# Dilated attention moved between the retention's projections, retention moved to the end, in the first mixers of a two-model kernel

## The chip, the cores and the metric

The kernel runs on one core of one Trainium2 chip, as one program with one launch. The metric is device time in microseconds, the median of several executions. The core has five engines that work side by side, each through its own instructions in program order, tied together by semaphores: TensorE (PE in the profile, matrix products; its weight loads are PEld), VectorE (DVE), ScalarE (ACT), GpSimd (POOL) and SyncE (SP), which here issues the DMAs.

## The reference

Two transformer models run one after the other on a sequence of 512 tokens of width 1024. The first has two layers (feed-forward, token mixer, feed-forward), the second two further layers of other kinds. The change touches the first model's token mixer alone, which runs twice, once in each layer:

```python
def _token_mixer(h, w_in, w_out):
    proj = h @ w_in
    rq, rk, rv, rg, dq, dk, dv, sq, sk, sv = jnp.split(proj, points, axis=-1)
    y_ret = _retention(_rotate(rq), _rotate(rk), rv, rg)      # 4 heads, 64 x 128
    y_dil = _dilated_attention(_rotate(dq), _rotate(dk), dv)  # 4 heads of 64
    y_sb = _stick_breaking(sq, sk, sv)                        # 4 heads of 64
    return jnp.concatenate([y_ret, y_dil, y_sb], -1) @ w_out
```

Retention is a decayed causal product without softmax, its output normed over each head's 128 columns and multiplied with `silu(rg)`. Dilated attention is a softmax over masked scores. Stick-breaking weights each value by running sums of log-sigmoids. All of it is in float32.

## The kernel before

Activations lie transposed, as eight tiles of 128 features by 512 tokens. Each large product is made of three passes, since both factors are parted into a high and a low half (`HH` and `HL` for the activations; ScalarE copies the high half, VectorE or GpSimd subtracts for the low one). Weights come in chunks of 256 columns: a DMA into a stage, the high half copied by ScalarE (`split`), the low one subtracted by VectorE (`low`). One chunk gives 48 products of 512 columns on TensorE.

The order of all work is written by a planner, class `Plan`, in plain Python before anything is emitted. It makes one list of steps; each engine's program is that list with the steps that concern it. Background work is written as generators ("units"): a unit yields between its steps. `self.tick()`, called after each half tile of a projection (12 products), starts up to `burst` new units from the queue `bg`, if fewer than `depth` are active, then waits `pace` ticks before it starts more, and moves every active unit one step on. A callable at the head of `bg` holds the queue until it gives true. `pipeline` ticks until all is done, with no projection between; `until(f)` ticks until `f()` holds.

`first_mixer` goes so. `late` makes the projections `sq` and `sk`; then follow the projection `sv`, and stick-breaking units in pairs of heads (`sb_z`, `sb_keep`, `sb_sum`, `sb_mask`, `sb_av`), one every second tick, beside `rq`, `rk` and `rv`. Then the gates `rg` (chunks 4 and 5), `dq`, `dk` and `dv` are projected, with eight retention units (`ret_s`, `ret_av`) and the retention's norm (`ret_norm`: squares `ret_sq`, column sums `ret_var`, root `ret_rs`, and for each head `ret_out`, which spreads the root over a PSUM bank and multiplies it in) beside them. Last, `self.pipeline(dil_units())` runs the 16 dilated units (`attend`: score and mask, `at_exp`, `at_norm`, `at_turn`, `at_av`), two a tick. Then `m_part` parts the tiles 6, 7 (stick-breaking) and 0 to 3 (retention); tiles 4 and 5 (dilated) are parted directly from PSUM by the last `at_av`. `project_out` makes the product with `w_out`, whose first chunk takes the eight tiles in the order 6, 7, 0 to 5, two per call of `mm2`. Its `take` also writes the split of the next weight chunk and, at this place, one chunk of the modulation's rows (`ada_rows`, VectorE, L2150 to L2156).

Lines of the profile: L1487 is every TensorE product, L1502 the spread, L1507 the transpose; L1814 every plain copy of ScalarE; L2137 `low`; L2130 and L2691 low halves of `HL` on VectorE and GpSimd; L2106 to L2125 the root; L2369 and L2760 the two multiplications of `ret_out` on VectorE and GpSimd; L1955 `ret_sq`; L2742 and L2755 the masks of `sb_keep` and `sb_mask`; L2402 `at_norm`.

Of the kernel before, what the change touches and what calls it, by code (L numbers as in the profile page):

```python
# [25 lines left out]
P = 128  # L26
# [79 lines left out]
class Plan:  # L106
# [216 lines left out]
                self.tick()  # L323
        return b, self.pid

    def feat2(self, ch, kt, x, ver, eager=False, n=S, order=None):
# [4 lines left out]
        yield from self.rest_of(*self.begin(ch, kt, n, x, ver, order))  # L331

    def begin(self, ch, kt, n, x, ver, order=None, wide=(P, P)):
        bs = [self.banks.take(), self.banks.take()]
        self.pid += 2
        return ch, self.pid - 1, kt, n, bs, x, ver, list(order or range(kt)), wide

    def rest_of(self, ch, pid, kt, n, bs, x, ver, ks, wide):

        for i in range(0, kt, 2):  # L340
            self.add("mm2", pid, ch, kt, n, bs, x, ver, ks, wide, i, i + 2)
            self.tick()
        yield bs[0], pid
        yield bs[1], pid + 1
# [279 lines left out]
            self.hv += 1  # L624
        return after or (total if mean != "rms" else self.squares(*total))

    def project_out(self, name, idx0, kt, nc, x, ver, gate, mean, order=None, nxt=None, raw=None):
        total, done, per = (self.new(), []), [], nc // P
        after = self.norm(*nxt) if nxt else None
        for c in range(NT // per):  # L630
            ch = self.take(name, idx0 + c, ada=c == 0)
            tiles = (self.feat2(ch, kt, x, ver, True, order=order) if per == 2 and c == 0 else
                     (self.feat(ch, kt, nc, t, x, ver) for t in range(per)))
# [40 lines left out]

    def first_mixer(self, l, norm):
        extra = [("xm", i) for i in range(3)]
        nk_done, sb_done, out_done, ropes = {}, [], {}, []

        def proj(idx, key):
            ch = self.take("w_in", l * 12 + idx, ada=False)  # L680
# [66 lines left out]
        def ret_unit(pr, j, cells):  # L747
            b, q = [], []
            for c in range(2):
                b.append(self.banks.take())  # L750
                q.append(self.tmp.take())
                self.banks.free(b[c], ("ret.d", l, 2 * pr + c, j))
            self.add("ret_s", l, pr, j, b, q)
            yield
            for c in range(2):
                if j == 0:
                    cells.append(self.held.take())
                self.add("ret_av", l, 2 * pr + c, j, cells[c], q[c])
                self.tmp.free(q[c], ("ret.o", l, 2 * pr + c, j))
                if j == 3:  # L760
                    self.held.free(cells[c], ("ret.kept", l, 2 * pr + c))
                    out_done[2 * pr + c] = True

        def ret_norm():
            yield
            st2 = self.held.take()
            prev = None
            for h in range(5):
                if h < 4:
                    q = self.tmp.take()  # L770
                    self.add("ret_sq", l, h, q)
                if prev is not None:
                    self.add("ret_var", l, h - 1, st2, prev)
                    self.tmp.free(prev, ("ret.var", l, h - 1))
                prev = q
                if h % 2:
                    yield
            y = self.yr.take()
            self.add("ret_rs", l, st2, y)
            self.held.free(st2, ("rs.v", "ret%d" % l))  # L780
            yield
            yield
            for h in range(4):
                b = self.banks.take()
                self.add("ret_out", l, h, y, b)
                self.banks.free(b, ("ret.out", l, h))
                yield
            self.yr.free(y, ("ret.sp2", l, 3))

        def ret_units():  # L790
# [3 lines left out]
                    yield ret_unit(pr, j, cells)  # L794
            yield ret_norm()

        def setpace(n):
            self.pace = n
            return True

        def dil_units():
            for pr in range(2):
                cell = []
                for i in range(4):
                    for c in range(2):
                        yield self.attend("dil", l, 2 * pr + c, i, (i + 1) * P, cell, i == 3 and c == 1)
# [8 lines left out]
        for i in extra:  # L815
            self.tmp.after[i] = [free]
        self.tmp.ids += extra
        tproj(11, "sv", 0)
        self.bg.extend(sb_units())
        self.pace = 2  # L820
        proj(0, "rq")
        proj(1, "rk")
        self.active += [roped("rq", "ret"), roped("rk", "ret")]
        tproj(2, "rv", 0)
        tproj(3, "rv", 256)
        self.bg.append(lambda: setpace(1))
        self.bg.append(lambda: len(ropes) >= 2 and len(sb_done) == 2)
        self.bg.extend(ret_units())
        for c in range(2):
            ch = self.take("w_in", l * 12 + 4 + c, ada=False)  # L830
            for t in range(2):
                b, pid = self.feat(ch, 8, 256, t, "h", hv, turn=False)
                self.add("m_gate", l, 2 * c + t, pid, b)
                self.banks.free(b, ("m.g", l, 2 * c + t))
                self.tick()
            self.release(ch, ("proj", pid))
        proj(6, "dq")
        proj(7, "dk")
        self.active += [roped("dq", "dil"), roped("dk", "dil")]
        self.hfree = tproj(8, "dv", 0)  # L840
        self.hv += 1
        self.burst, self.depth = 2, 8
        self.bg.append(lambda: len(ropes) == 4)
        self.pipeline(dil_units())
        self.burst, self.depth = 1, 6
# [10 lines left out]
    def attend(self, kind, l, h, i, n, cell, last, free=None):  # L856

        u = (kind, l, h, i)
        b, q, sm = self.banks.take(), self.tmp.take(), self.small.take()
# [19 lines left out]
        if last:  # L879
            o = cell[0]  # L880
            if kind == "x":
                self.held.free(o, ("o.lo", l, h), ("o.hi", l, h))
            else:
                self.held.free(o, ("h.lo", self.hv, 4 + h // 2), ("h.hi", self.hv, 4 + h // 2))

# [924 lines left out]
def scalar(e, m, plan):  # L1810
    act = e.i

    def copy(out, src):
        return act.activation(out, src, ACT.Copy)  # L1814
# [103 lines left out]
    def m_gate(l, h, pid, b):  # L1918
        e.wait_ge(("proj", pid))
        act.activation(m.t["rg"][:, h, :], m.bank(b), ACT.Silu).then_inc(*e.up("act_evict", "m.g", l, h))  # L1920

    def sb_z(l, pr, j, z, q):
# [32 lines left out]
        act.activation(m.tmp(q), m.ret(h), ACT.Square).then_inc(*e.up("act_sq", "ret.sq", l, h))  # L1955

    def m_part(l, n, odd, hv, hfree):
        e.wait_ge(("sb.kept", l, n - 6) if n >= 6 else ("ret.out", l, n), hfree)
        copy(m.HH[:, n, :], m.mixed(n)).then_inc(*e.up("act_h", "h.hi", hv, n))


# [11 lines left out]
    def at_av(u, n, p, o, last, hv, hfree):  # L1973
        if last and u[0] == "x":
            e.wait_ge(("at.o", u), hfree)
            copy(m.OH[:, u[2], :], m.bank(o)).then_inc(*e.up("act_h", "o.hi", u[1], u[2]))
        elif last:
# [119 lines left out]
def vector(e, m, plan):  # L2097
# [248 lines left out]
    def m_center(l, i, c0):  # L2346
        v = m.t["rv"][:, i:i + 2, c0:c0 + 256].rearrange("p a (g n) -> p a g n", n=P)
        total = m.RM[:, 0:4].rearrange("p (a g) -> p a g", a=2)
        e.wait_ge(("m.v", l, "rv", c0, i))
# [54 lines left out]
    def at_av(u, n, p, o, last, hv, hfree):  # L2404
        if last and u[0] == "x":
            e.wait_ge(("o.hi", u[1], u[2]))
            dve.tensor_tensor(m.OL[:, u[2], :], m.bank(o), m.OH[:, u[2], :].bitcast(F32), ALU.subtract).then_inc(
                *e.up("dve_h", "o.lo", u[1], u[2]))
        elif last:
            h_low(hv, 4 + u[2] // 2, m.bank(o))  # L2410


# [433 lines left out]
class Mem:  # L2846
# [105 lines left out]
    def first_mixer(self):  # L2952
        at = self.parts(("sq", [2, S]), ("sk", [2, S]), ("sv", [4, 256]), ("rq", [2, S]), ("rk", [2, S]), ("nk", [2, 1280]),
                        ("rv", [4, S]), ("rg", [4, S]), ("dq", [2, S]), ("dk", [2, S]), ("dv", [4, 256]))
        self.spare("xm", 3, at)

    def even_mixer(self):
        at = self.parts(("qi", [2, S]), ("ki", [S]), ("bm", [1152]), ("wi", [4, 4]), ("st", [4, 18]),
# [83 lines left out]
        return self.t["nk"][:, :, :].rearrange("p a n -> p (a n)")[:, h * S:(h + 1) * S]  # L3042

    def mixed(self, n):
        return self.t["rg"][:, n, :] if n < 4 else self.t["sq"][:, n - 6, :]

    def tile(self, key, t):
        if key == "ki":
# [209 lines left out]
```

## Time and profile before

| | |
|---|---|
| runs | 3520.28, 3524.86, 3524.43 us; median 3524.43 |
| profiled execution | 3520.2 us from the first to the last instruction; no time beside the span is given for it |
| TensorE busy | 3433.7 us, 98% |
| VectorE, ScalarE, GpSimd busy | 1894.9, 1198.5 and 519.9 us |
| chain that ended last | TensorE 34% of the span, nearly all of it L1487 |

A busy share near 100% on one engine means that the length of its own instructions sets the time. Matmul durations overlap in the records, since they are pipelined: the distance from start to start is what one costs (0.23 us for 512 columns at the full clock, 0.43 at half). PEclk is the granted clock as a share of 2.4 GHz.

### The profile page before, as it was taken

To read this page: it belongs to the slowest core of one execution; us is meant where nothing else is said; L and a number is where in the kernel's file an instruction comes from. 1 tells how busy PE (TensorE), PEld (TensorE's weight loads), DVE (VectorE), ACT (ScalarE), POOL (GpSimd) and SP (SyncE) were. 2 spreads that over 40 slices of the span, in tenths; PEclk is the share of its full clock that TensorE was granted. 3 is DMA by queue.
4 is the path that set the end of the run, shared out by engine and by line. 5 is a ranking of instruction groups with operands and counts; after the bars stand their busy time and mean duration, and the time that the engine had idled before them with its cause. 6 is when DMAs were issued, how large, how long until landed. Compare 5 with 4: busy or idle time off the path is not lost. (4 is left out here: it accounts for less than half of the span.)

```text
span 3520.2 us, 40510 instructions
## 1 busy us (share of the span) xinstructions
PE 3433.7 (98%) x16478; PEld 2789.2 (79%) x16478; DVE 1894.9 (54%) x3227; ACT 1198.5 (34%) x1646; POOL 519.9 (15%) x454
## 2 busy tenths in 40 slices
PE   8999999999999999999999999989999999999999
PEld 5888876688888888876788877757888888878887
DVE  5555753664556455744752346885643345564433
ACT  3222352442224222453442234445432222352221
POOL 1010231210012010231210021112011110211111
PEclk9999999999999999999999999979999999999999
DMA  6444221133442444211132212101222222322221
GB/s 264 178 180 179 92 77 60 49 144 144 168 144 108 155 156 161 93 58 48 63 142 96 96 66 84 60 13 61 73 96 96 96 96 99 108 73 96 96 96 72
DMA packets 53036, 372.53 MB, mean 106 GB/s; under 512 B 6001, under 2 KB 6129, under 8 KB 10098
## 3 DMA queue, kind: packets, MB, share of 16 engines
q1 hardware_dynamic: 52850, 369.94, 28.8%
q8 instruction: 130, 2.13, 0.2%
q14 instruction: 56, 0.46, 0.0%
HBM read 367.82 MB, written 2.10 MB: 105 GB/s over the span
## 5 line engine op out<-in xcount | busy, mean ns | idle before, releaser
L1487 PE MATMUL ps<-s_hh,s_wh 128*128 128x512 f32 x2552 | 1012.8, 397 | 18.8 <-POOL s_hl L2691 14.1
L1487 PE MATMUL ps<-s_hh,s_wl 128*128 128x512 f32 x2552 | 998.3, 391 | 0.0
L1487 PE MATMUL ps<-s_hl,s_wh 128*128 128x512 f32 x2552 | 998.0, 391 | 0.0
L2137 DVE TENSOR_TENSOR s_wl<-s_stage,s_wh 128x2048 fp32r<-128x2048 f32 (+1 forms) x276 | 623.5, 2259 | 635.3 <-ACT s_wh L1814 635.3
L1814 ACT ACTIVATE s_wh<-s_stage 128x2048 fp32r<-128x2048 f32 (+1 forms) x276 | 519.2, 1881 | 586.0 <-PE ps L1487 427.0
L1487 PEld LDWEIGHTS ps<-s_hh,s_wh 128*128 128x128 f32 x2552 | 481.7, 189 | 138.9 <-issue 34.9
L1487 PEld LDWEIGHTS ps<-s_hh,s_wl 128*128 128x128 f32 x2552 | 481.7, 189 | 102.7
L1487 PE MATMUL ps<-s_ah,s_wh 128*128 128x512 f32 x1408 | 561.9, 399 | 0.7 <-POOL s_al L2730 0.7
L1487 PEld LDWEIGHTS ps<-s_hl,s_wh 128*128 128x128 f32 x2552 | 482.5, 189 | 98.0 <-issue 0.7
L1487 PE MATMUL ps<-s_ah,s_wl 128*128 128x512 f32 x1408 | 550.1, 391 | 0.0
L1487 PE MATMUL ps<-s_al,s_wh 128*128 128x512 f32 x1408 | 549.5, 390 | 0.0
L2730 POOL TENSOR_TENSOR s_al<-s_tmp,s_ah 128x512 fp32r<-128x512 f32 x152 | 197.5, 1303 | 1665.9 <-ACT s_ah L1814 1665.9
L1487 PEld LDWEIGHTS ps<-s_ah,s_wl 128*128 128x128 f32 x1408 | 264.3, 188 | 57.4
L1487 PEld LDWEIGHTS ps<-s_ah,s_wh 128*128 128x128 f32 x1408 | 264.6, 188 | 54.9 <-POOL s_al L2730 1.6
L1487 PEld LDWEIGHTS ps<-s_al,s_wh 128*128 128x128 f32 x1408 | 264.7, 188 | 53.6 <-issue 1.9
L1814 ACT ACTIVATE s_ah<-s_tmp 128x512 fp32r<-128x512 f32 x152 | 95.9, 632 | 562.0 <-DVE s_tmp L2320 302.8
L2197 DVE TENSOR_TENSOR s_xr<-ps,s_xr 128x512 f32<-128x512 f32 x96 | 66.1, 689 | 196.8 <-PE ps L1487 196.8
L2153 DVE SCALAR_TENSOR_TENSOR s_tmp<-s_stage,s_cond,s_tmp 128x256 f32<-128x256 f32 x384 | 157.3, 478 | 0.0
L2195 DVE SCALAR_TENSOR_TENSOR s_xr<-ps,s_sm,s_xr 128x512 f32<-128x512 f32 x112 | 83.0, 748 | 114.1 <-PE ps L1487 113.5
L1842 ACT ACTIVATE s_tmp<-ps 128x512 f32<-128x512 f32 x82 | 48.8, 596 | 251.4 <-PE ps L1487 251.4
L2320 DVE TENSOR_TENSOR s_tmp<-s_tmp,ps 128x512 f32<-128x512 f32 x82 | 55.6, 684 | 113.1 <-PE ps L1487 111.8
L2304 DVE TENSOR_TENSOR s_tmp<-ps,s_c 128x512 f32<-128x512 f32 x64 | 44.0, 688 | 118.5 <-PE ps L1487 105.1
(502 smaller groups left out, 3614.7 us busy)
## 6 DMA issues: line engine op xcount, KB each, us to landing
s_stage<-in_w_ada SPq DMA_DIRECT2D x64, 1024.0 KB, 4.8
s_stage<-in_ffn_w_gate SPq DMA_DIRECT2D x44, 1024.0 KB, 4.8
s_stage<-in_ffn_w_up SPq DMA_DIRECT2D x44, 1024.0 KB, 4.8
s_stage<-in_ffn_down SPq DMA_DIRECT2D x32, 1024.0 KB, 4.8
s_stage<-in_w_up SPq DMA_DIRECT2D x32, 1024.0 KB, 4.7
s_stage<-in_down_m SPq DMA_DIRECT2D x32, 1024.0 KB, 4.7
s_stage<-in_w_in SPq DMA_DIRECT2D x24, 1024.0 KB, 4.8
s_stage<-in_ffn_down SPq DMA_DIRECT2D x16, 768.0 KB, 4.3
```

The source lines that it names most:

```text
L1487: return pe.matmul(out, lhs, rhs, start=start, stop=stop, skip_group_check=True)
L1814: return act.activation(out, src, ACT.Copy)
L1842: act.activation(m.tmp(q), m.bank(b), ACT.Silu).then_inc(*e.up("act_ffn", "act", pid))
L2137: ins = dve.tensor_tensor(m.wl(ws)[:, a:z], m.STAGE[:, j % NS, a:z], m.wh(ws)[:, a:z].bitcast(F32), ALU.subtract)
L2153: ins = dve.scalar_tensor_tensor(dst, w[:, k, :], cond, dst, ALU.mult, ALU.add)
L2195: ins = dve.scalar_tensor_tensor(x, m.bank(b), m.small(gate[0])[:, n:n + 1], x, ALU.mult, ALU.add)
L2197: ins = dve.tensor_tensor(x, m.bank(b), x, ALU.add)
L2304: dve.tensor_tensor(x, m.bank(b), m.RB, ALU.mult).then_inc(*e.up("dve_act", "act", pid))
L2320: dve.tensor_tensor(m.tmp(q), m.tmp(q), m.bank(b), ALU.mult).then_inc(*e.up("dve_ffn", "glu", pid))
L2730: pool.tensor_tensor(m.AL[a][:, k, :], m.tmp(q), m.AH[a][:, k, :].bitcast(F32), ALU.subtract).then_inc(*e.up("pool_a", "a.lo", av, k))
```

## The change

The mixer's projections are reordered to `sv`, `dq`, `dk`, `dv`, `rq`, `rk`, `rv`, gates. The dilated units start beside `rq`, at two a tick; the retention units beside the gates; the retention's norm is run after the last gate product. The output product's first chunk takes the tiles in the order 6, 7, 4, 5, 0, 1, 2, 3, and `rest_of` waits in the plan for each pair to be parted. The gates' space serves as four more temporaries until the gates are written. A retention cell takes a rotating PSUM bank where no held one is free. The dilated output is copied to `dq` and parted later.

```diff
-    def rest_of(self, ch, pid, kt, n, bs, x, ver, ks, wide):
+    def rest_of(self, ch, pid, kt, n, bs, x, ver, ks, wide, ready=None):
         for i in range(0, kt, 2):
+            if ready:
+                self.until(lambda: ready(ks[i]) and ready(ks[i + 1]))
             self.add("mm2", pid, ch, kt, n, bs, x, ver, ks, wide, i, i + 2)
             self.tick()
...
                 if j == 0:
-                    cells.append(self.held.take())
+                    ring = self.held if self.held.spare() else self.banks
+                    cells.append((ring, ring.take()))
...
+            rooted.append(y)
             yield
             yield
             for h in range(4):
                 b = self.banks.take()
                 self.add("ret_out", l, h, y, b)
                 self.banks.free(b, ("ret.out", l, h))
-                yield
+                self.add("m_part", l, h, h % 2, self.hv, self.hfree)
+                parted.append(h)
+                if h % 2:
+                    yield
...
         tproj(11, "sv", 0)
         self.bg.extend(sb_units())
-        self.pace = 2
+        self.depth = 5
+        proj(6, "dq")
+        proj(7, "dk")
+        self.active += [roped("dq", "dil"), roped("dk", "dil")]
+        tproj(8, "dv", 0)
+        self.bg.append(lambda: len(ropes) >= 2 and pacing(1, 2, 9))
+        self.bg.extend(dil_units())
         proj(0, "rq")
         proj(1, "rk")
         self.active += [roped("rq", "ret"), roped("rk", "ret")]
         tproj(2, "rv", 0)
         tproj(3, "rv", 256)
-        self.bg.append(lambda: setpace(1))
-        self.bg.append(lambda: len(ropes) >= 2 and len(sb_done) == 2)
+        self.bg.append(lambda: len(ropes) == 4 and len(sb_done) == 2 and len(dil_done) >= 1 and pacing(1, 1, 9))
         self.bg.extend(ret_units())
...
-        proj(6, "dq")
-        proj(7, "dk")
-        self.active += [roped("dq", "dil"), roped("dk", "dil")]
-        self.hfree = tproj(8, "dv", 0)
+        self.hfree = ("proj", pid)
         self.hv += 1
-        self.burst, self.depth = 2, 8
-        self.bg.append(lambda: len(ropes) == 4)
-        self.pipeline(dil_units())
-        self.burst, self.depth = 1, 6
-        order = (6, 7, 0, 1, 2, 3, 4, 5)
-        for i, n in enumerate(order[:6]):
+        self.until(lambda: len(dil_done) == 2)
+        order = (6, 7, 4, 5, 0, 1, 2, 3)
+        for i, n in enumerate(order[:4]):
             self.add("m_part", l, n, i % 2, self.hv, self.hfree)
+        self.until(lambda: rooted)
...
         norm = self.project_out("w_out", l * 4, 8, 256, "h", self.hv, gate, "ln", order,
-                                (l, 1, (l, 6, 7), None))
+                                (l, 1, (l, 6, 7), None), ready=lambda n: n in parted or n >= 4)
+        self.pace, self.burst, self.depth = 1, 1, 6
```

`pacing(pace, burst, depth)` sets the three and gives true. `attend` gets a list `done`, to which a dilated pair of heads adds itself at its last unit.

## Rows read from the trace of the kernel before

**Rows 1.** The page, part 1: TensorE's busy time and instructions.

```profile
PE 3433.7 (98%) x16478; PEld 2789.2 (79%) x16478; DVE 1894.9 (54%) x3227; ACT 1198.5 (34%) x1646; POOL 519.9 (15%) x454
```

**Rows 2.** Table of windows of 50 us: busy of each engine, clock, DMA.

```profile
600.00:650.00 50.00, 42.26 (x290) 30.80 (x289) 35.20 (x93) 26.16 (x62) 14.58 (x10) 0.93 0.06 22
...
1650.00:1700.00 50.00, 42.55 (x251) 30.38 (x250) 36.77 (x97) 26.33 (x62) 9.35 (x6) 0.93 0.12 43
...
2700.00:2750.00 50.00, 50.00 (x223) 41.38 (x222) 17.89 (x17) 9.70 (x7) 2.59 (x2) 1.00 0.30 106
```

**Rows 3.** TensorE's waits, 451.9 to 658.8 us: total, times, longest.

```profile
PE ps L1507 <- DVE s_tmp L2402: 3.4, 3, 2.2
PE ps L1487 <- POOL s_hl L2691: 2.6, 1, 2.6
PE ps L1487 <- POOL s_xm L2755: 2.1, 1, 2.1
```

**Rows 4.** Timeline of TensorE, dilated stage: start, duration, operation, [idle before <- releaser].

```profile
617.05 1.03 PE L1502 MATMUL ps<-s_cc,s_ny 128*128 128x128 f32 x8
...
621.57 0.72 PE L1507 MATMUL ps<-s_cc,s_tmp 128*128 128x128 f32 x2 [2.20 <-DVE s_tmp L2402]
...
636.51 1.13 PE L1487 MATMUL ps<-s_dk,s_dq 64*128 64x512 f32 x4
...
641.49 0.65 PE L1507 MATMUL ps<-s_cc,s_tmp 128*128 128x128 f32 x4
642.07 2.23 PE L1487 MATMUL ps<-s_tmp,s_dv 128*64 128x128 f32 x28
646.95 0.77 PE L1487 MATMUL ps<-s_hh,s_wh 128*128 128x512 f32 x1 [2.65 <-POOL s_hl L2691]
```

**Rows 5.** Timeline of TensorE, the retention's norm beside the projection `dk`.

```profile
590.47 1.05 PE L1487 MATMUL ps<-s_cc,s_tmp 128*128 128x1 f32 x8 [1.21 <-ACT s_tmp L1955]
591.38 0.48 PE L1487 MATMUL ps<-s_hh,s_wh 128*128 128x512 f32 x1
...
595.81 1.84 PE L1487 MATMUL ps<-s_cc,s_tmp 128*128 128x1 f32 x16
597.51 0.47 PE L1487 MATMUL ps<-s_hh,s_wh 128*128 128x512 f32 x1
...
600.36 0.95 PE L1487 MATMUL ps<-s_cc,s_tmp 128*128 128x1 f32 x8
```

**Rows 6.** Timeline around a late stick-breaking mask: GpSimd, VectorE, TensorE.

```profile
528.59 0.46 POOL L2742 TENSOR_TENSOR s_nk<-s_nk,s_cc 128x128 f32<-128x128 f32 x1 [2.49 <-DVE s_tmp L2337]
529.91 2.43 POOL L2742 TENSOR_TENSOR s_nk<-s_nk,s_cc 128x128 f32<-128x128 f32 x1 [0.87 <-DVE s_tmp L2337]
...
529.75 2.28 DVE L2137 TENSOR_TENSOR s_wl<-s_stage,s_wh 128x2048 fp32r<-128x2048 f32 x1
...
532.81 1.33 PE L1487 MATMUL ps<-s_xm,s_sv 128*64 128x384 f32 x4 [2.05 <-POOL s_xm L2755]
```

**Rows 7.** Timeline of VectorE: root, multiplication, weight half, modulation's rows.

```profile
601.35 0.18 DVE L2106 TENSOR_SCALAR s_nv<-ps 128x16 f32<-128x16 f32 x1 [14.75 <-PE ps L1487]
...
603.45 0.17 DVE L2125 SCALAR_TENSOR_TENSOR s_ny<-s_nu,s_ny 128x16 f32<-128x16 f32 x1
...
607.65 0.69 DVE L2369 TENSOR_TENSOR s_rg<-s_rg,ps 128x512 f32<-128x512 f32 x1 [1.82 <-PE ps L1502]
...
651.56 2.28 DVE L2137 TENSOR_TENSOR s_wl<-s_stage,s_wh 128x2048 fp32r<-128x2048 f32 x1
653.77 0.61 DVE L2150 TENSOR_SCALAR s_tmp<-s_stage,s_cond 128x256 f32<-128x256 f32 x2
...
656.78 0.42 DVE L2156 TENSOR_TENSOR s_tmp<-s_tmp 128x256 f32<-128x256 f32 x1
```

**Rows 8.** Timeline of ScalarE: the retention's four squares.

```profile
589.79 2.18 ACT L1955 ACTIVATE s_tmp<-s_nk 128x512 f32<-128x512 f32 x4
```

**Rows 9.** Timeline of GpSimd: one gate product of the retention.

```profile
568.01 1.28 POOL L2760 TENSOR_TENSOR s_rg<-s_nk,s_rg 128x512 f32<-128x512 f32 x1 [26.72 <-ACT s_nk L1814]
```

More of the change, by code:

```diff
@@ L324, in feat, with feat2 @@
         return b, self.pid
-    def feat2(self, ch, kt, x, ver, eager=False, n=S, order=None):
+    def feat2(self, ch, kt, x, ver, eager=False, n=S, order=None, ready=None):
         if not eager:
@@ L330, in feat2 @@
             return
-        yield from self.rest_of(*self.begin(ch, kt, n, x, ver, order))
+        yield from self.rest_of(*self.begin(ch, kt, n, x, ver, order), ready)
     def begin(self, ch, kt, n, x, ver, order=None, wide=(P, P)):
@@ L625, in ffn, with project_out @@
         return after or (total if mean != "rms" else self.squares(*total))
-    def project_out(self, name, idx0, kt, nc, x, ver, gate, mean, order=None, nxt=None, raw=None):
+    def project_out(self, name, idx0, kt, nc, x, ver, gate, mean, order=None, nxt=None, raw=None, ready=None):
         total, done, per = (self.new(), []), [], nc // P
@@ L631, in project_out @@
             ch = self.take(name, idx0 + c, ada=c == 0)
-            tiles = (self.feat2(ch, kt, x, ver, True, order=order) if per == 2 and c == 0 else
+            tiles = (self.feat2(ch, kt, x, ver, True, order=order, ready=ready) if per == 2 and c == 0 else
                      (self.feat(ch, kt, nc, t, x, ver) for t in range(per)))
@@ L676, in first_mixer @@
         extra = [("xm", i) for i in range(3)]
-        nk_done, sb_done, out_done, ropes = {}, [], {}, []
+        gates = [("xg", i) for i in range(4)]
+        sb_done, dil_done, out_done, ropes, rooted, parted = [], [], {}, [], [], []
         def proj(idx, key):
@@ L756, in ret_unit @@
                 if j == 0:
-                    cells.append(self.held.take())
-                self.add("ret_av", l, 2 * pr + c, j, cells[c], q[c])
+                    ring = self.held if self.held.spare() else self.banks
+                    cells.append((ring, ring.take()))
+                ring, cell = cells[c]
+                self.add("ret_av", l, 2 * pr + c, j, cell, q[c])
                 self.tmp.free(q[c], ("ret.o", l, 2 * pr + c, j))
                 if j == 3:
-                    self.held.free(cells[c], ("ret.kept", l, 2 * pr + c))
+                    ring.free(cell, ("ret.kept", l, 2 * pr + c))
                     out_done[2 * pr + c] = True
@@ L795, in ret_units, with pacing @@
             yield ret_norm()
-        def setpace(n):
-            self.pace = n
+        def pacing(pace, burst, depth):
+            self.pace, self.burst, self.depth = pace, burst, depth
             return True
@@ L805, in dil_units @@
                     for c in range(2):
-                        yield self.attend("dil", l, 2 * pr + c, i, (i + 1) * P, cell, i == 3 and c == 1)
+                        yield self.attend("dil", l, 2 * pr + c, i, (i + 1) * P, cell, i == 3 and c == 1, None, dil_done)
         one, two, free = self.late(norm, (("w_in", l * 12 + 9), ("w_in", l * 12 + 10)))
@@ L814, in first_mixer @@
         hv = self.hv
-        for i in extra:
+        for i in extra + gates:
             self.tmp.after[i] = [free]
-        self.tmp.ids += extra
+        self.tmp.ids += extra + gates
         tproj(11, "sv", 0)
         self.bg.extend(sb_units())
-        self.pace = 2
+        self.depth = 5
[5 more added lines that the diff above has]
+        self.bg.extend(dil_units())
         proj(0, "rq")
@@ L825, in first_mixer @@
         tproj(3, "rv", 256)
-        self.bg.append(lambda: setpace(1))
-        self.bg.append(lambda: len(ropes) >= 2 and len(sb_done) == 2)
+        self.bg.append(lambda: len(ropes) == 4 and len(sb_done) == 2 and len(dil_done) >= 1 and pacing(1, 1, 9))
         self.bg.extend(ret_units())
+        self.tmp.ids = [i for i in self.tmp.ids if i not in gates]
         for c in range(2):
@@ L832, in first_mixer @@
                 b, pid = self.feat(ch, 8, 256, t, "h", hv, turn=False)
-                self.add("m_gate", l, 2 * c + t, pid, b)
+                self.until(lambda: ("xg", 2 * c + t) not in self.tmp.busy)
+                self.add("m_gate", l, 2 * c + t, pid, b, self.tmp.after[("xg", 2 * c + t)])
                 self.banks.free(b, ("m.g", l, 2 * c + t))
@@ L851, in first_mixer, with attend @@
         norm = self.project_out("w_out", l * 4, 8, 256, "h", self.hv, gate, "ln", order,
-                                (l, 1, (l, 6, 7), None))
+                                (l, 1, (l, 6, 7), None), ready=lambda n: n in parted or n >= 4)
+        self.pace, self.burst, self.depth = 1, 1, 6
         self.small.free(gate[0], ("x", NT - 1, self.xv[NT - 1]))
         return norm
-    def attend(self, kind, l, h, i, n, cell, last, free=None):
+    def attend(self, kind, l, h, i, n, cell, last, free=None, done=None):
         u = (kind, l, h, i)
@@ L882, in attend @@
                 self.held.free(o, ("o.lo", l, h), ("o.hi", l, h))
+            elif kind == "dil":
+                self.held.free(o, ("dil.kept", l, h // 2))
+                done.append(h // 2)
             else:
@@ L1916, in m_tcopy, with m_gate @@
             *e.up("act_evict", "m.v", l, key, c0, i))
-    def m_gate(l, h, pid, b):
-        e.wait_ge(("proj", pid))
+    def m_gate(l, h, pid, b, free):
+        e.wait_ge(("proj", pid), free)
         act.activation(m.t["rg"][:, h, :], m.bank(b), ACT.Silu).then_inc(*e.up("act_evict", "m.g", l, h))
@@ L1957, in m_part @@
     def m_part(l, n, odd, hv, hfree):
-        e.wait_ge(("sb.kept", l, n - 6) if n >= 6 else ("ret.out", l, n), hfree)
+        e.wait_ge(("sb.kept", l, n - 6) if n >= 6 else ("dil.kept", l, n - 4) if n >= 4 else ("ret.out", l, n), hfree)
         copy(m.HH[:, n, :], m.mixed(n)).then_inc(*e.up("act_h", "h.hi", hv, n))
@@ L1976, in at_av @@
             copy(m.OH[:, u[2], :], m.bank(o)).then_inc(*e.up("act_h", "o.hi", u[1], u[2]))
+        elif last and u[0] == "dil":
+            e.wait_ge(("at.o", u))
+            copy(m.t["dq"][:, u[2] // 2, :], m.bank(o)).then_inc(*e.up("act_evict", "dil.kept", u[1], u[2] // 2))
         elif last:
@@ L2348, in m_center @@
         total = m.RM[:, 0:4].rearrange("p (a g) -> p a g", a=2)
-        e.wait_ge(("m.v", l, "rv", c0, i))
+        e.wait_ge(("m.v", l, "rv", c0, i), ("m.c", l, c0, 0) if i else ("m.c", l, 0, 2) if c0 else None)
         dve.tensor_reduce(total, v, AXX, ALU.add).then_inc(*e.up("dve_ret", "m.total", l, c0, i))
@@ L2408, in at_av @@
                 *e.up("dve_h", "o.lo", u[1], u[2]))
-        elif last:
+        elif last and u[0] == "b":
             h_low(hv, 4 + u[2] // 2, m.bank(o))
@@ L2955, in first_mixer @@
         self.spare("xm", 3, at)
+        for k in range(4):
+            self.extra["xg", k] = self.t["rg"][:, k, :]
     def even_mixer(self):
@@ L3044, in mixed @@
     def mixed(self, n):
-        return self.t["rg"][:, n, :] if n < 4 else self.t["sq"][:, n - 6, :]
+        return self.t["rg"][:, n, :] if n < 4 else self.t["dq"][:, n - 4, :] if n < 6 else self.t["sq"][:, n - 6, :]
     def tile(self, key, t):
```

## The prediction

> **What bounds the kernel now.** I read the page first. The TensorE row [rows 1] shows 98% busy: everywhere outside a few stages the time is the length of the row of matmuls, so a reordering can only win what TensorE loses now, as idle time or at the half clock. The table of 50 us windows says where that is: in most windows, as in the last one quoted, TensorE is busy for 50.00 of 50; the two that hold the dilated attention, one for each of the two first mixers, show 42.26 and 42.55 at a granted clock of 0.93 [rows 2]. TensorE's waits in the first mixer's stretch name the rest: softmax (`s_tmp` L2402), the low half of the mixed rows (`s_hl` L2691), one stick-breaking mask (`s_xm` L2755) [rows 3]. The two mixers' windows differ by 0.3 us of busy time [rows 2], so I work out one and double it.
>
> A ledger of what TensorE loses in a mixer before, beyond the work itself:
>
> - Dilated stage. It runs from 617.05 (two spreads of the retention, 1.0 us) to the first output product at 646.95: 29.9 us [rows 4]. Its own TensorE work: eight pairs of scores, 1.13 us at 512 columns and in proportion below, so (4+3+2+1)/4 x 1.13 x 2 = 5.7; 40 transposes at 0.65/4 = 6.5; 80 value records at 2.23/28 = 6.4; together 18.6. Lost: 29.9 - 1.0 - 18.6 = 10.3.
> - Retention norm. 1.2 us idle at 590.47, then twelve products take 4.43 us (591.38 to 595.81), where the next twelve take 2.85 (597.51 to 600.36) [rows 5]: the clock had fallen to its lower level after the gap, 1.6 more. Lost: 2.8.
> - Stick-breaking: 2.05 us idle [rows 6], and one slow piece like the one above, estimated at 1.6 too: 3.7.
>
> Sum 16.8 us a mixer, 33.6 in all: the most that the change could win, about 1%.
>
> **The change, part by part.** The planner gives one background turn ("tick") for each half tile of projection, twelve products, 2.85 us [rows 5]. I followed the ticks from the first tick after the late tiles.
>
> *Middle.* The value projection `sv` has ticks 1 to 4, `dq`, `dk`, `dv` 5 to 16, `rq`, `rk`, `rv` 17 to 32, the gates 33 to 40. With pace 1 and depth 5 (the scaling unit takes a place until tick 10) stick-breaking units start at ticks 5 to 8, 11, 12, 14 and 16. Dilated units start at 17, two a tick; the last value product falls at tick 31. The retention can start only when `rv` is queued, at 33, last unit at 40. So all 18.6 us of dilated work lie between products of `rq`, `rk` and `rv`. They are eight ticks of two units: TensorE has 2.85 us of product and 18.6/8 = 2.3 of dilated work in each, 5.2 in all. The window that holds the whole stage has VectorE busy for 35.20 us and ScalarE for 26.16 [rows 2], so by an upper bound 4.4 and 3.3 us a tick, below 5.2. The 10.3 us go away. The stick-breaking units, now one a tick, keep their chain; the bounds for their stall are 0, if the products of the next unit cover it, and 3.7 for each as before (a rival). Following the queues I get a slip of some tenths at one mask and set 0.3.
>
> Instruction counts stay, also the DMA issues and their order relative to the chunks; fewer switches of ScalarE's table are off TensorE's path. The copy of the dilated output to `dq` is new in place of the direct high/low copy, but it lies beside products: nothing. The four low halves beside the gates' end: same durations as before, and not the last to come (below).
>
> *Tail.* Here the retention norm has no projection beside it any more. Let T be the end of the last gate product. On TensorE follow value products, scores, value products of the last units: 1.8 us, ending at about T+2.4. ScalarE, in order: the gate 0.6, four `m_part` copies at 0.54 (the shape of the squares), two kept copies, four squares (2.18 for four) [rows 8]: the first square ends at T+4.3. Four statistics cost 0.9 + 1.7 + 0.8 = 3.4 [rows 5], so they end at T+7.8. Idle so far 2.6.
>
> Then two blocks of output products (tiles 6, 7 and 4, 5, ready long before): 5.5 us to T+13.3, two spreads to 14.2. Beside them VectorE does the root, 2.3 us [rows 7], to T+10.1, seven small coefficient instructions (about 1, estimated at 0.15 each from the root's), the low half of the next weight chunk 2.2, and the modulation's rows, 653.77 to 657.20, 3.4 [rows 7]: these are written by `take` ahead of `ret_out`, in the order of the program. So VectorE reaches the first `ret_out` only at T+16.7. What is queued behind those rows is the multiplication, and for it wait ScalarE's copy, GpSimd's low half, TensorE's product of tile 0. The chain: multiplication 0.7 [rows 7], copy 0.6, low half on GpSimd 1.28, by an instruction of its shape [rows 9], so tile 0 at T+19.4: idle 5.1. GpSimd's gate product for head 1 stands behind that low half: 1.28 + 0.7 + 0.6 + 0.7 (VectorE's own low half) give T+22.8, less 1.4 of product: idle 2.0. The spreads of heads 2 and 3 stand behind those products: 0.5 + 0.7 + 0.6 + 1.28, 2.2 idle beyond the spreads; then head 3 as head 1: 1.9. The block ends at T+32. Idle: 2.6 + 5.1 + 2.0 + 2.2 + 1.9 = 13.8.
>
> The clock: no row shows such a row of gaps. Below: it never falls, 0. Above: every piece of about 3 us of work runs slow, four at 1.6 = 6.4. The dilated stage before is the nearest, the window holding it at 0.93 [rows 2]; I take two pieces, 3.2.
>
> **Sum.** After: 13.8 + 3.2 + 0.3 = 17.3; before 16.8; +0.5 a mixer, +1 in both. Against the profiled execution, span 3520.2, that is 3521.2; the median of the runs stands 4.2 above that span, so 3525.4. The ledger leaves out small slow pieces after the old gaps (some 1 us a mixer, which the change removes), so I say 3524. In words: what is won in the middle is given back in the tail.
>
> **Rivals.**
>
> *Faster, the clock holds in the tail.* The gaps are 2 us with 1.4 us of product between; row 590.47 shows a drop after 1.2 us idle plus thin statistics, which speaks against it; that in the old stage only part of 30 us was slow speaks for it. Slow 0 and middle 0: 13.8 against 16.8 + 1, so -4 a mixer, -8: 3516. With the 5.1 gap shorter too, as the rows may come while the statistics still run, down to -8 a mixer: 3508.
>
> *Slower, masks late in the middle.* Before, the mask that stalled TensorE stood behind a GpSimd instruction of 0.46 us that took 2.43, at the same time as VectorE's weight low half of 2.28 [rows 6]. With pace 1 there is a mask each tick beside the same weight halves. Each such stall is 3.7. The tail alone is 17.0; slower by over 7 us needs 17.0 + 3.7n > 17.8 + 3.5, so two stalls a mixer decide. Two: +6.6 a mixer, 3538; one: 3530. Against it: where before only every second tick started a unit, the ticks between a sum and its value product now hold another unit's products too, which cover a mask.
>
> The Trainium skill, "SBUF — State Buffer", section "SBUF: two separate sides", has the pair of ports that VectorE and GpSimd share as an exclusive lock, by which a VectorE instruction with two SBUF inputs blocks GpSimd wholly while it lasts. The trace agrees (0.46 grew to 2.43, by about the 2.28 beside it). By it each mask that meets a weight half is 2 us late; without it, it would be on time, and this rival would have no mechanism.
>
> *The change doesn't do what it says:* dilated units not done by the end of the gates. The count gives nine ticks of slack; 2 in 100.
>
> **Chances.** Under 0.2% (7 us) a measurement of this kernel tells no difference. Forecast, within 0.2%: 0.38. Clock holds or a shorter tail, faster: 0.34. Slower: 0.28, of it masks 0.15, a tail with all pieces slow (+3.7 a mixer, 3531) 0.11, not hidden 0.02. The range takes in both bounds of the clock and two masks nearly: 3508 to 3537. The likeliest case's own range is 3518 to 3531.
>
> **What would show it.** In the profile after: no stretch without projections between `dv` and the gates, and TensorE busy over 95% there; retention records beside the gate products; then, from the last gate product, about 32 to 36 us to the end of the first output chunk, with a wait of 5 us for `s_hl` after the block of tiles 4 and 5 and three of 2 us. VectorE's modulation rows (L2153) directly before the first multiplication at L2369. If that first wait is below 2 us the tail is mis-sized and the kernel is faster; if a mask wait (L2755) appears more than once a mixer, the slower rival holds. What would make me wrong most easily is the tail: it is one chain through four engines, each link with about 0.1 us of latency that I read off but did not sum twice.

## The result, and the profile after

| | before | after |
|---|---|---|
| median of the runs, us | 3522.36 (3517.81 to 3524.86) | 3543.50 (3540.51 to 3547.82) |
| profiled execution, span, us | 3520.2 | 3539.2 |
| ratio of the medians | | 1.006, 95% interval 1.0048 to 1.0072 |

The kernel became 21 us slower; 3524 was forecast, with 3537 as the upper end. The median stands 4.3 us above the profiled span: each run's time is 1.3 us above its own span, and the profiled run was the shortest of the four. Before, the forecast's 4.2 us came about in the same way, from three runs; with the fourth run the median of before is 3522.36, 2.2 us above its profiled span.

Part 1 of the page of the kernel after, to be held against [rows 1]:

```profile
PE 3448.9 (97%) x16478; PEld 2796.5 (79%) x16478; DVE 1890.8 (53%) x3225; ACT 1190.3 (34%) x1642; POOL 511.0 (14%) x456
```

The same 16478 matmuls are busy for 15 us longer, and no other engine has more to do: the matmuls ran at a lower clock for longer. Windows of the kernel after; the first and the third are two of [rows 2], the second is the one that follows the first, the last four cut the first mixer at 515, 530 and 632 us:

```profile
core 0: us, PE busy (x) PEld busy (x) DVE busy (x) ACT busy (x) POOL busy (x), PEclk, DMA share, GB/s
600.00:650.00 50.00, 47.74 (x208) 34.37 (x208) 22.65 (x51) 12.20 (x18) 4.62 (x3) 0.93 0.16 57
650.00:700.00 50.00, 43.48 (x169) 34.22 (x169) 23.43 (x24) 13.01 (x14) 13.99 (x11) 0.86 0.19 70
1650.00:1700.00 50.00, 46.30 (x203) 33.35 (x201) 21.84 (x50) 12.41 (x19) 4.63 (x3) 0.93 0.18 64
...
451.00:515.00 64.00, 62.82 (x311) 43.36 (x310) 30.86 (x51) 40.68 (x79) 20.23 (x36) 1.00 0.14 50
515.00:530.00 15.00, 12.04 (x38) 8.38 (x37) 8.09 (x19) 3.96 (x12) 5.07 (x6) 0.77 0.20 70
530.00:632.00 102.00, 102.00 (x571) 74.05 (x570) 44.74 (x89) 33.63 (x63) 5.98 (x6) 1.00 0.15 52
632.00:670.00 38.00, 29.23 (x113) 22.49 (x112) 17.16 (x41) 10.76 (x17) 10.85 (x8) 0.73 0.15 56
```

From 530 to 632 TensorE has no gap: all the dilated work and the retention lie between products, and the stage of [rows 4] and the gap of [rows 5] are gone. Two places lose. One, from 632 on, is the tail that the prediction reckoned. The other is the 15 us from 515 on, at a clock of 0.77, where it reckoned 0.3 us. TensorE's waits in the first mixer after:

```profile
PE ps L1502 <- POOL s_hl L2709: 5.0, 2, 2.6
PE ps L1502 <- DVE s_tmp L2355: 3.7, 3, 3.0
PE ps L1502 <- ACT s_xm L1970: 1.9, 1, 1.9
PE ps L1502 <- DVE s_hl L2148: 1.6, 2, 0.9
PE ps L1502 <- DVE s_rg L2355: 0.5, 1, 0.5
PE ps L1502 <- DVE s_tmp L2378: 0.4, 1, 0.4
```

L2355 is VectorE's second instruction of `sb_keep`, the last reader of the PSUM banks of a stick-breaking score. No wait names the mask (now L2773), nor does one in the second mixer.

Three marks cut a mixer: the first stick-breaking score; T, the start of the value products that follow the last gate product; and the first `w_out` tile taken from PSUM by VectorE (`s_xr`). All times in us, first and second mixer; before has other work ahead of its last gate product, so that only the sum compares:

| kernel | first score to T | T to first output tile | sum |
|---|---|---|---|
| before | | | 204.0, 200.2 |
| after | 178.6, 178.6 | 35.5, 34.8 | 214.1, 213.4 |

The sums grow by 10.1 and 13.2, 23.3 together. The spans of the same two executions differ by 19.0 and the medians by 21.1, so the two mixers account for the loss. What is left of the span outside the two stretches is 3116.0 us before and 3111.6 after; in the profiles of all the kernels below it lies between 3110.6 and 3122.3, though the edits hardly reach it. I don't know why, and it limits what a comparison of single profiles can say.

### The profile page after: what moved, and what is told of

It reads as the page before. It is cut to its first block, busy times and chain, and to the rows that moved or that the text cites. A ratio compares the mean times of both kernels' runs of the same rounds, so it can differ in the third digit from the quotient of the medians.

```text
span 3539.2 us, 40520 instructions
## 1 busy us (share of the span) xinstructions
PE 3448.9 (97%) x16478; PEld 2796.5 (79%) x16478; DVE 1890.8 (53%) x3225; ACT 1190.3 (34%) x1642; POOL 511.0 (14%) x456
## 4 chain that ended last, share of the span: by engine, by line
PE 44%; DVE 4%; ACT 1%; issue 1%; POOL 0%; DVEq 0%; ACTq 0%; POOLq 0%
PE ps L1502 44%; PE ps L1522 0%; DVE s_sm L2555 0%; DVE s_bm L2557 0%; DVE s_wl L2155 0%; ACT s_wh L1829 0%; DVE s_hl L2148 0%; DVE s_xr L2287 0%; DVE s_xx L2420 0%; DVE s_sm L2418 0%; PE ps L1517 0%; DVE s_sm L2398 0%; DVE s_tmp L2420 0%; DVE s_tmp L2277 0%; ACT s_xx L1981 0%
```

## The middle: VectorE frees a bank late

TensorE of the kernel after, from the first two dilated units on (their scores, then twelve products, most of them left out here, then the next two scores):

```profile
516.54 0.49 PE L1502 MATMUL ps<-s_dk,s_dq 64*128 64x128 f32 x2
519.99 0.79 PE L1502 MATMUL ps<-s_dk,s_dq 64*128 64x128 f32 x2 [2.96 <-DVE s_tmp L2355]
520.71 0.79 PE L1502 MATMUL ps<-s_hh,s_wh 128*128 128x512 f32 x1
521.30 0.63 PE L1502 MATMUL ps<-s_hl,s_wh 128*128 128x512 f32 x1
521.73 0.63 PE L1502 MATMUL ps<-s_hh,s_wl 128*128 128x512 f32 x1
...
526.13 1.45 PE L1502 MATMUL ps<-s_dk,s_dq 64*128 64x256 f32 x4
527.51 0.50 PE L1502 MATMUL ps<-s_hh,s_wh 128*128 128x512 f32 x1
```

The score of the second dilated unit waits 2.96 us for a PSUM bank; then the next products start 0.43 us apart instead of 0.23, the lower of the two clock levels, until 526. VectorE in that time:

```profile
515.39 2.29 DVE L2155 TENSOR_TENSOR s_wl<-s_stage,s_wh 128x2048 fp32r<-128x2048 f32 x1 [4.78 <-ACT s_wh L1829]
517.60 1.01 DVE L2361 TENSOR_TENSOR s_rg<-s_rg,ps 128x384 f32<-128x384 f32 x2
518.53 0.68 DVE L2353 SCALAR_TENSOR_TENSOR s_nk<-ps,s_tmp 128x512 f32<-128x512 f32 x1
519.24 0.69 DVE L2355 TENSOR_TENSOR s_tmp<-ps,s_nk 128x512 f32<-128x512 f32 x1
```

It stood idle for 4.78 us at the head of its queue, for a high half of weights that ScalarE copied only after the softplus of the newest unit (that ended at 513.0), then made the low half, then `sb_sum` (L2361); `sb_keep` (L2353, L2355), whose input had been there since 513.0, came third. Its first half ended at 519.93 and TensorE moved at 519.99. The second mixer has the same wait, of 2.96 us at 1568.54.

GpSimd at the same moment: an addition of `sb_sum` (L2767) beside VectorE's weight half, then a mask of `sb_keep` (L2760):

```profile
515.62 3.33 POOL L2767 TENSOR_TENSOR s_nk<-s_nk 128x256 f32<-128x256 f32 x2 [3.63 <-PE ps L1502]
520.02 0.45 POOL L2760 TENSOR_TENSOR s_nk<-s_nk,s_cc 128x128 f32<-128x128 f32 x1 [1.06 <-DVE s_tmp L2355]
```

Of the eight instructions of that line in a mixer the median is 0.59 us and the longest, one of these two, 2.64. That is again what the Trainium skill, "SBUF — State Buffer", section "SBUF: two separate sides", says of the pair of ports: VectorE's weight half began first, at 515.39, and the addition grew by the 2.06 us of it that were left. But GpSimd was then 1.06 us idle for VectorE: the long addition cost TensorE nothing. The collision that the slower rival asked for took place, and nobody waited for it.

## Experiments

Each edits the kernel after. "Before" was run beside each set.

**1. Hold the dilated units until the eight `sb_keep` are queued** (`sb_kept` collects them).

```diff
-        self.bg.append(lambda: len(ropes) >= 2 and pacing(1, 2, 9))
+        self.bg.append(lambda: len(ropes) >= 2 and len(sb_kept) == 8 and pacing(1, 2, 9))
```

> The changed kernel, with one more condition on the first dilated unit: it starts only in the tick after the last sb_keep is in the plan. Theory A (the second dilated score waits 2.96 us for a PSUM bank that the last stick-breaking unit frees only when VectorE has reached its sb_keep behind a weight half, and the clock falls after it): the wait and the slow products behind it go, about 6 us a mixer, 12 in all, 3531. Rival B (VectorE and ScalarE are late as a whole, the bank is only where it shows): the wait comes back at another score, transpose or mask, less than 2 us a mixer gained, 3540 or more.

Measured: 3555.5 (3554.0 to 3556.8), 1.0095 (1.0079 to 1.0112): slower than the kernel after. The wait at the second score fell to 0.2 and 0.8 us, and others came, for copies of ScalarE:

```profile
PE ps L1504 <- ACT s_rv L1831: 2.6, 2, 2.2
...
PE ps L1524 <- ACT s_rq L1831: 0.7, 1, 0.7
PE ps L1524 <- ACT s_rk L1831: 0.5, 1, 0.5
```

This is rival B, and worse than it said: starting dilated units later moves the waits onto `rq`, `rk` and `rv`. A mixer takes 216.5 us, 2.4 and 3.1 more than in the kernel after; the rest of the 12 us by the medians lies outside the two stretches and stays unexplained. A later start of the dilated units alone doesn't win the loss back.

**2. Retention units two a tick**, so that the norm's statistics come beside the last gates.

```diff
-        ... len(dil_done) >= 1 and pacing(1, 1, 9))
+        ... len(dil_done) >= 1 and pacing(1, 2, 9))
```

> The changed kernel with two retention units a tick in place of one, so that squares, statistics and root of the retention's norm come beside the last gate products. Theory A (the norm left without cover costs the tail its idle time and the slow products after it): from the last gate product to the spreads 16.8 us become about 8, and the 5 us of work taken out lie beside products: 3 to 4 us a mixer less, 7 in all, 3536. Rival B (the tail is set by VectorE's weight half and modulation rows before the first ret_out): no gain, 3542 to 3544.

Measured: 3546.5 (3544.4 to 3549.3), 1.0069 (1.0054 to 1.0084). The statistics did come earlier, the first at 627.40 instead of 636.63 and beside the last gate products, and still the first retention tile waited:

```profile
654.07 0.80 PE L1502 MATMUL ps<-s_hh,s_wh 128*128 128x512 f32 x1 [4.42 <-POOL s_hl L2709]
```

VectorE's weight half and modulation rows (645.77 to 651.40) stand directly before the first multiplication there as well. This is rival B: earlier squares win nothing while these rows and the chain behind them stay. The two mixers take 214.3 and 214.0 us.

**3. The tail without its chain**: all four `ret_out`, then all four `m_part`, and the modulation's rows one chunk later. The first multiplication also comes one tick sooner, after twelve products of output instead of 24.

```diff
-            yield
-            yield
+            yield
             for h in range(4):
                 ...
                 self.banks.free(b, ("ret.out", l, h))
+            for h in range(4):
                 self.add("m_part", l, h, h % 2, self.hv, self.hfree)
                 parted.append(h)
-                if h % 2:
-                    yield
...
-            ch = self.take(name, idx0 + c, ada=c == 0)
+            ch = self.take(name, idx0 + c, ada=c == (1 if ready else 0))
```

> The changed kernel; the four ret_out come together after the first output block, their four m_part behind them, and the modulation's rows one chunk later. Theory A (the tail is one chain a head through VectorE, ScalarE, GpSimd and TensorE, run four times in series): the waits of 2.6, 0.7, 2.3 and 0.9 us and the slow products between them go, 9 to 11 us a mixer, about 20 in all, 3523. Rival B (the chain only shifts, since low halves on GpSimd take 1.3 us each and gate products as much): half of that, 3533.

Measured: 3521.0 (3517.0 to 3523.1), before 3522.4, 0.9993 (0.9984 to 1.0002): 22.5 us less than the kernel after. Its tail, T at 630.85:

```profile
635.26 2.94 PE L1500 MATMUL ps<-s_cc,s_xm 128*128 128x1 f32 x16 [1.88 <-ACT s_xm L1968]
638.06 3.55 PE L1500 MATMUL ps<-s_cc,s_tmp 128*128 128x1 f32 x16
641.47 0.77 PE L1500 MATMUL ps<-s_hh,s_wh 128*128 128x512 f32 x1
...
646.51 1.91 PE L1515 MATMUL ps<-s_cc,s_ny 128*128 128x128 f32 x16
648.18 0.48 PE L1500 MATMUL ps<-s_hh,s_wh 128*128 128x512 f32 x1
...
656.86 0.47 PE L1500 MATMUL ps<-s_hh,s_wh 128*128 128x512 f32 x1 [0.26 <-DVE s_xr L2211]
```

This is theory A. After the four spreads 36 products run with no wait for a low half; T to the output tile is 25.1 us instead of 35.5. The two stretches are 22.5 us shorter together, as the medians are.

**4. Fill the gap ahead of the statistics** with two full-width products into a free bank, whose result nobody reads.

```diff
             yield
+            wb = self.banks.take()
+            self.add("warm", l, wb)
+            self.banks.free(wb, ("warm", l))
             st2 = self.held.take()
...
```

> The changed kernel with two extra full-width products into a free bank (results unused) in the 1.9 us gap before the retention's first statistic. Theory A (the clock falls from that gap, and the slow blocks of tiles 6, 7, 4, 5 are hidden by VectorE's rows anyway): the 24 products run faster, 8.4 us to 5.5 to 7, the wait for tile 0 grows by as much, time within 2 us of the changed kernel. Rival B (the slow products set the end): 3 us a mixer less, 3537. Rival C (the thin statistics drop the clock, whatever is before them): products still at 0.43 us each, time the same.

Measured: 3542.6 (3532.7 to 3547.4), 1.0054 (1.0033 to 1.0075), no difference from the kernel after that these four runs can show. In the first mixer the 24 products took 7.1 instead of 7.9 us (seven of them still 0.43 us apart), and the wait for tile 0 behind them grew from 2.62 to 3.39. What the faster products won, the wait took: the slow clock in these products costs nothing of its own. The slow clock in the statistics before them does. Measured from the end of the statistics, where the 24 products begin, tile 0 begins 11.6 us later in both mixers of the kernel after and of 1, 4, 5 and 9, however fast the products between are. The statistics ended at T+8.9 and T+9.5 in the kernel after and at T+8.0 and T+9.0 here, so that tile 0 began 0.9 and 0.5 us sooner.

**5. Another bank for the dilated score**: the even head's takes a held bank where one is spare, so that it need not wait for `sb_keep`.

```diff
-        b, q, sm = self.banks.take(), self.tmp.take(), self.small.take()
+        ring = self.held if kind == "dil" and h % 2 == 0 and self.held.spare() else self.banks
+        b, q, sm = ring.take(), self.tmp.take(), self.small.take()
...
```

> The changed kernel; the first head's dilated score of each pair takes one of the two held PSUM banks where one is free, so that the second head's takes the rotating bank that the first used. Theory A (the wait of 2.96 us at the second dilated score is for the one bank, and the clock falls after it): both go, 5 to 6 us a mixer, 3532. Rival B (VectorE and ScalarE, each bound to its order, are late at this place; the holding of the first unit by a tick only moved the waits): the wait returns at another bank or tile within two ticks, under 2 us a mixer gained, 3540 or more.

Measured: 3543.4 (3532.1 to 3546.2), 1.005 (1.0034 to 1.0066). The 2.96 us went, and in its place:

```profile
523.64 0.70 PE L1503 MATMUL ps<-s_dk,s_dq 64*128 64x256 f32 x4 [1.54 <-DVE s_sm L2413]
```

besides 0.8 us each for `s_sq` and `s_rq` of ScalarE. The medians show no gain, as rival B had it. In the profile the waits ahead of T are about as long in sum (4.6 us against 4.1 in the first mixer), but no twelve products run slow, and first score to T is 175.7 and 175.6 us, 2.9 less a mixer. That execution was the shortest of five (span 3530.8), so its gain is not the typical one; whether the bank wins 2 or 3 us a mixer stays open.

**6 to 8. Combinations.** 6 is the edits of 5 and 3; 7 adds that of 2; 8 is 3 with the rows left where they were, before the first multiplication.

> The held bank and the four ret_out together with the modulation's rows one chunk later. If the two losses add up and the bank theory holds: 3521 less 10, 3511. If only the tail counts: 3520 to 3522.

> The one before, with two retention units a tick besides, so that the norm lies beside the last gate products. Theory A (with VectorE's rows out of the way the uncovered norm is what is left of the tail, 1.9 us idle and slow products after it): 3 to 5 us a mixer less than without it, 3503 if the bank theory holds, 3513 if not. Rival B (retention pairs or the low halves that wait for the last gate product take it back): no gain over the one before.

> The changed kernel with the four ret_out together, the modulation's rows left where they are, before the first ret_out on VectorE. Theory A (the serial chain is the larger part): 3 us a mixer worse than with the rows later, 3527. Theory B (the rows ahead of the first multiplication are the larger part, as the step of the prediction with 5.1 us has it): 3533 or more.

Measured: 6: 3524.1 (3516.8 to 3525.2), 0.9997 (0.9988 to 1.0007). 7: 3524.4 (3520.3 to 3530.6), 1.0002 (0.9992 to 1.0011). 8: 3528.5 (3524.0 to 3532.3), 1.001 (1.0 to 1.0019). By the medians, grouping the steps gives 15 us from the kernel after (8), moving the rows 7.5 more (3); which is near theory A's 3527 for 8; held banks and pairs add nothing that the medians show, against the 3511 and 3503 that their theories gave. The 7.5 is less sure than the 15: 3 and 8 were run in different sets, and each against before of its own set they are 6.1 apart; T to output tile differs by 0.9 and 1.1 us only, first score to T, which the edit doesn't touch, by 1.2 in both mixers.

**9. Stick-breaking units every second tick again**, with the depth of before, 6 instead of 5.

```diff
-        self.depth = 5
+        self.pace = 2
         proj(6, "dq")
```

> Stick-breaking units start every second tick again (pace 2, depth as before), all else as in the changed kernel. The changed kernel loses 2.96 us at the second dilated score, then runs 12 products at 0.43 us, some 7 to 8 us from the first stick-breaking score to the last gate product in each mixer. Theory A: it is the density of stick-breaking units that makes their banks come free late; with every second tick VectorE reaches each sb_keep in time, the 2.96 us wait goes, 4 to 7 us a mixer come back, about 3531 to 3536. Theory B: the wait follows from what stands before the dilated units' start (weight halves, rotations) and not from the density; the units end later and now lie beside the first dilated ones, so a wait of the same size stays or moves: 3540 to 3548, about the changed kernel's 3543.5.

Measured: 3531.0 (3524.1 to 3534.3), before 3523.0, 1.0023 (1.0014 to 1.0032): 12.5 us less than the kernel after. The stretch that had a clock of 0.77:

```profile
451.00:515.00 64.00, 64.00 (x323) 46.48 (x322) 32.36 (x51) 38.55 (x74) 19.96 (x32) 1.00 0.18 66
515.00:530.00 15.00, 14.89 (x65) 9.85 (x64) 7.26 (x13) 7.91 (x15) 6.93 (x10) 1.00 0.06 9
```

No wait names `sb_keep` any more, in either mixer. First score to T is 169.6 us in both mixers, 9.0 less. Theory A: the density was the cause. The edit changes the depth too and brings the first dilated score 71.8 us after the first stick-breaking score instead of 62.9. The later start alone did not help (1); the depth was not tried alone. The profiled execution (3524.1) was the shortest of eleven, so its stretches are those of a short one.

**10. Both: 9 and 3.**

> Pace 2 as in the run before it, together with the joined tail (four multiplications, then the four partings in a row, and the modulation's rows a chunk later). The joined tail alone gave 3520.97 against 3522.4 of the kernel before. Theory A: both gains add, 3520.97 less 7 to 12 us, 3509 to 3514: faster than both kernels. Theory B: the middle keeps its loss, 3518 to 3524, no difference from the kernel before.

Measured: 3508.7 (3507.0 to 3510.5), before 3523.0, 0.996 (0.9947 to 0.9972). It is faster than both kernels, by 14 and by 35 us, and slightly below the lower bound of the range that its theory gave. TensorE's waits in the first mixer are down to three:

```profile
PE ps L1500 <- ACT s_tmp L1968: 1.9, 1, 1.9
PE ps L1500 <- DVE s_tmp L2376: 0.4, 1, 0.4
PE ps L1500 <- DVE s_xr L2211: 0.3, 1, 0.3
```

The table of stretches, with these (first and second mixer):

| kernel | first score to T | T to first output tile | sum |
|---|---|---|---|
| 3, tail without chain | 177.4, 177.4 | 25.1, 25.1 | 202.5, 202.5 |
| 8, as 3, rows kept | 178.6, 178.6 | 26.0, 26.2 | 204.6, 204.7 |
| 9, every second tick | 169.6, 169.6 | 34.2, 36.5 | 203.8, 206.1 |
| 10, both | 169.6, 169.6 | 25.1, 23.5 | 194.8, 193.2 |

## Why the prediction was wrong, point by point

**The ledger of before** held for the first mixer and was doubled without looking: the second lost 3.9 us less. Its late mask is there too, 2.1 us, but nothing after it ran slow; nor did the twelve products behind the 1.2 us of the retention norm, 2.87 us in the second mixer where [rows 5] has 4.43:

```profile
525.00:540.00 15.00, 12.95 (x44) 8.11 (x43) 8.33 (x11) 7.26 (x9) 4.92 (x7) 0.89 0.19 70
...
1562.00:1577.00 15.00, 12.95 (x51) 8.77 (x50) 9.28 (x12) 8.89 (x10) 5.92 (x8) 1.00 0.19 71
...
1631.39 0.49 PE L1487 MATMUL ps<-s_hh,s_wh 128*128 128x512 f32 x1
...
1634.26 0.95 PE L1487 MATMUL ps<-s_cc,s_xm 128*128 128x1 f32 x8
```

All rows are of the kernel before. Same gap at the mask, clock 0.89 and 1.00. The two places give 1.6 us each; the other 0.7 lies in small steps. So before lost 16.8 + 12.9 = 29.7, not 33.6. The two windows quoted from before, which differed by 0.3, covered neither place.

**Dilated stage and retention norm gone from the middle**: right, with the tick count (530 to 632 us above).

**Middle, "a slip of some tenths at one mask and set 0.3"**: this is the step that failed. Against the same stretch at pace 2 it cost 9.0 us a mixer: waits of 1.2 for banks up to 515 and of 2.96 at 517, the twelve products that follow 5.3 us long instead of 2.85, the score after them 1.45 instead of 0.70 (the same form in 5). That is 7.4; the other 1.6 lie in small steps that I did not assign. The 9.0 depends on the clock: with the same wait first score to T took between 175.9 and 178.7 us in the profiles of 3, 4, 8 and the kernel after, 6.3 to 9.1 above pace 2. The rival for it named the mask; it was VectorE, not GpSimd, that came late, and a bank, not a value, that TensorE wanted. The count of busy microseconds a tick (4.4 and 3.3 by an upper bound, "below 5.2") was right on average and said nothing: 8.09 of 15 us of VectorE were busy while TensorE waited for it, because a weight half with its own wait stood ahead. The argument that another unit's products would cover a mask was right for masks; the same new unit also took two more banks and put its softplus ahead of ScalarE's weight copy.

**Tail**: the total was right, 32 + 3.2 against 35.5 and 34.8, but by luck: in the first mixer TensorE was idle for 8.8 us instead of 13.8, and slow work cost 8.5 instead of 3.2. The tail of the kernel after:

```profile
638.43 2.82 PE L1502 MATMUL ps<-s_cc,s_tmp 128*128 128x1 f32 x16
...
649.02 1.04 PE L1517 MATMUL ps<-s_cc,s_ny 128*128 128x128 f32 x8
652.67 0.62 PE L1502 MATMUL ps<-s_hh,s_wh 128*128 128x512 f32 x1 [2.62 <-POOL s_hl L2709]
656.08 0.79 PE L1502 MATMUL ps<-s_hh,s_wh 128*128 128x512 f32 x1 [0.66 <-DVE s_hl L2148]
658.81 1.49 PE L1517 MATMUL ps<-s_cc,s_ny 128*128 128x128 f32 x8
662.64 0.50 PE L1502 MATMUL ps<-s_hh,s_wh 128*128 128x512 f32 x1 [2.34 <-POOL s_hl L2709]
666.06 0.80 PE L1502 MATMUL ps<-s_hh,s_wh 128*128 128x512 f32 x1 [0.90 <-DVE s_hl L2148]
```

The waits are those of the chain, in its order and on its engines: 2.62, 0.66, 2.34, 0.90, where 5.1, 2.0, 2.2, 1.9 were written. They are shorter because the products between them ran slow; 4 shows that the one fills the other. I added idle time and slow clock as if they were separate, and the sum came out since the slow part had been set too low (7.9 us for the first 24 products alone, 2.4 more than 5.5). The chain from the statistics to tile 0 was right: from T+7.8 to T+19.4 it was reckoned as 11.6 us, and 11.6 it took, beginning at T+8.9 since the statistics ran slow. That the modulation's rows end directly before the first multiplication was right too:

```profile
647.11 2.45 DVE L2171 SCALAR_TENSOR_TENSOR s_tmp<-s_stage,s_cond,s_tmp 128x256 f32<-128x256 f32 x6
649.60 0.42 DVE L2174 TENSOR_TENSOR s_tmp<-s_tmp 128x256 f32<-128x256 f32 x1
649.94 0.68 DVE L2387 TENSOR_TENSOR s_rg<-s_rg,ps 128x512 f32<-128x512 f32 x1
```

**The sum, mended**: 2 x (17.3 + 9.0 - 0.3) = 52.0, less 29.7, gives +22.3; the stretches gave 23.3, the spans 19.0 and the medians 21.1. Without the middle's error, 34.6 - 29.7 = +4.9, where 9, which has no such loss, measured +8.0 (+5.6 in its stretches). The rivals: "clock holds" fell (0.73 in the tail); "masks late" gave a size near the truth, 3538 for two stalls a mixer, by another mechanism; "all pieces slow" in the tail came true for the clock, but the waits shrank by about as much, so that it cost nothing beyond the tail as reckoned (its 3531 leaves out the 1 us a mixer that the other rivals count; with it, 3530); "not hidden" did not occur.

## What to carry to other kernels

When background work is started twice as often, a mean busy share per tick can't say that the helpers keep up: follow the queue of each in order, and for each new unit ask which PSUM banks it takes and behind what long instruction the one that frees them stands. Where several tiles pass through the same four engines one after another, put all the steps of one kind together: the grouping alone gave 15 us here by the medians, one tick sooner included. Where a chain behind some work sets the end, look at when that work ends and not at how fast TensorE fills the wait. And before doubling a ledger, read the second copy of the stage.

## What the runs showed of the hardware

After 2.96 us idle, with the small products of a stick-breaking unit just ahead, twelve products ran at the lower clock level (0.43 us apart). That the clock falls there is likely and not sure. The same wait, 2.92 to 2.96 us, stands in ten mixers of the profiles (the kernel after, 2, 3, 4 and 8): in six all twelve products behind it were slow, in three the first half of them, and in the first mixer of 4 none (2.6 us from the start of the first to the start of the last, against 4.9). Before, after 2.05 us at the mask and after 1.2 us at the norm, the fall came in the first mixer and not in the second. In 5 a wait of 1.54 us left the products after it at full rate. In the tail the slow clock cost nothing in the products that a later wait followed, and its full price in the statistics that the chain started from (4).
